# One layer kernel: transposes from DMA back to TensorE, and a last tile whose second FFN half, gate and final norm go block by block

## Time and profile before

| | |
|---|---|
| median of 3 runs | 3140.91 us (3126.2 to 3141.65) |
| profiled execution: time | 3140.91 us |
| its span, slowest core (core 4) | 3139.2 us |
| spans of the 8 cores | 3113.1 to 3139.2 us |
| TensorE busy (matmuls) | 3069.9 us, 98% of the span |
| VectorE, ScalarE, GpSimd busy | 58%, 37%, 21% |
| DMA | 659 MB, mean 210 GB/s |

### The profile page before, as it was taken

The page is one execution under the profiler, slowest core; times in us unless marked ns, Lnnn a source line. Parts: engine busy times, 40 slices in busy tenths (PEclk is TensorE's granted clock), DMA queues, the critical chain, the costliest instruction groups (busy, mean ns, idle before and its releaser), DMA issues.

```text
span 3139.2 us, 46426 instructions; the slowest of 8 cores (3113.1 to 3139.2 us)
## 1 busy us (share of the span) xinstructions
PE 3069.9 (98%) x15344; PEld 1438.5 (46%) x15344; DVE 1834.3 (58%) x3681; ACT 1150.9 (37%) x1781; POOL 654.5 (21%) x601
## 2 busy tenths in 40 slices
PE   5999998999999999999999999999999999999998
PEld 2444444444444444444444444444444444444443
DVE  4755655746657376564746657375564746656344
ACT  4563534423333343333323333342333323332333
POOL 2421301411313022130212313022130312313000
PEclk8789999999999999999999999999999999999999
DMA  8858684755767657666665667657666665766552
GB/s 266 239 177 278 218 258 141 269 169 194 225 210 245 193 194 234 204 226 190 232 199 201 230 203 247 191 192 236 204 226 191 226 206 199 231 195 209 183 184 81
DMA packets 280248, 659.07 MB, mean 210 GB/s; under 512 B 179536, under 2 KB 179792, under 8 KB 229840
## 3 DMA queue, kind: packets, MB, share of 16 engines
q1 hardware_dynamic: 280016, 656.11, 64.9%
HBM read 554.32 MB, written 60.82 MB: 196 GB/s over the span
## 4 chain that ended last, share of the span: by engine, by line
PE 95%; DMA 2%; DVE 1%; issue 1%; ACT 1%; POOL 0%; DVEq 0%; SPq 0%; ACTq 0%; POOLq 0%
PE ps L625 92%; DMA stage<-wf 1%; PE ps L633 1%; DMA stage<-xT 1%; PE ps L949 0%; PE ps L813 0%; PE ps L777 0%; PE ps L815 0%; PE ps L825 0%; DMA stage<-wple 0%; ACT xsb L645 0%; DVE scr L727 0%; DVE scr L724 0%; DVE scr L730 0%; DMA xb<-x 0%
## 5 line engine op out<-in xcount | busy, mean ns | idle before, releaser
L625 PE MATMUL ps<-TG,ring 128*128 128x512 bf16 x5120 | 1160.9, 382 | 31.2 <-ACT ring L581 25.7
L625 PE MATMUL ps<-ring,TG 128*128 128x512 bf16 x4096 | 982.1, 385 | 11.3 <-DVE xb L1006 4.4
L625 PE MATMUL ps<-ring,hT 128*128 128x512 bf16 x4096 | 921.6, 379 | 0.0
L625 PEld LDWEIGHTS ps<-TG,ring 128*128 128x128 bf16 x5120 | 501.6, 98 | 633.7 <-issue 56.4
L625 PEld LDWEIGHTS ps<-ring,TG 128*128 128x128 bf16 x4096 | 402.7, 99 | 497.0 <-issue 65.1
L1069 DVE TENSOR_TENSOR hT<-rel 128x512 bf16<-128x512 f32 x491 | 404.2, 824 | 380.1 <-ACT rel L1065 375.6
L625 PEld LDWEIGHTS ps<-ring,hT 128*128 128x128 bf16 x4096 | 396.0, 98 | 456.4
L1065 ACT ACTIVATE rel<-ps 128x512 f32<-128x512 f32 x512 | 305.1, 596 | 711.2 <-PE ps L625 702.2
L733 POOL TENSOR_TENSOR qk<-scr 128x512 bf16<-128x512 f32 x128 | 174.5, 1363 | 1245.7 <-DVE scr L730 1245.7
L1092 DVE SCALAR_TENSOR_TENSOR xb<-ps,st,xb 128x512 f32<-128x512 f32 x288 | 214.8, 746 | 289.0 <-PE ps L625 285.8
L645 ACT ACTIVATE xsb<-xb 128x1024 bf16<-128x1024 f32 x200 | 210.2, 1051 | 367.7 <-DVE xb L1092 240.7
(11 more groups left out here) (79 smaller groups left out, 2014.4 us busy)
## 6 DMA issues: line engine op xcount, KB each, us to landing
ring<-wb SPq DMA_DIRECT2D x366, 1024.0 KB, 6.6
stage<-wf SPq DMA_DIRECT2D x104, 512.0 KB, 8.9
stage<-xT SPq DMA_DIRECT2D x64, 512.0 KB, 8.3
xb<-x SPq DMA_DIRECT2D x64, 512.0 KB, 8.3
out<-xb SPq DMA_DIRECT2D x64, 512.0 KB, 4.7
stage<-x SPq DMA_DIRECT2D x56, 512.0 KB, 11.6
wb<-ring SPq DMA_DIRECT2D x26, 1024.0 KB, 9.9
rot<-ROT SPq DMA_DIRECT2D x16, 512.0 KB, 6.0
```

Of the source, the lines that this page charges most:

```text
L625: r = e.matmul(out(), lhs(k), rhs(k), start=(start + k == 0), stop=(start + k == total - 1))
```

## The change

1. The DMA way of transposing is removed (`dmaT`, and its uses in `yT`, `outproj` and `gate`): all tiles take the TensorE way that tiles 0 to 2 took.
2. The limit `DMA_AHEAD` in the scheduler's model is removed: a DMA is taken as soon as SyncE, its inputs and its buffers are free.
3. Pools: `xsb` 4 to 2 buffers, `scr` 8 to 9, `st` 14 to 16. `sqsum` takes an `xsb` buffer of its own for its unused output; before, in `norm_T`, it wrote into the buffer that the cast then filled.
4. Last tile only (t = 15): in the second part of its FFN all four `w2` units are loaded first, and the groups go block by block (for each block both halves of the columns) where they went unit by unit. Its gate goes block by block as well, both halves of a block after each other, with the inverse norm of each block worked out by itself.
5. Last tile only: the add of the gated term is on VectorE alone, the square of the last norm is taken in halves of 512 columns, the last scaling is two instructions of 512 columns, and each half has a store of its own (256 KB).
6. In all gates the two matmuls of `p @ w_ple` are added before the eight of the gate, and they now also name the block's transposed residual as an input.
7. `gate(1)` starts at virtual time 306, not 290.

```diff
-DMA_AHEAD = 6.0
...
-                    if op.dma is not None and dma_free[0] > now + DMA_AHEAD:
-                        heapq.heappush(events, dma_free[0] - DMA_AHEAD)
-                        continue
...
-... qk=8, v=4, svn=2, ktok=2, PT=2, y=8, xsb=4, pT=1, stage=4,
-                rot=1, rel=3, gt=2, scr=8, st=14, psum=8, Sbf=2)
+... qk=8, v=4, svn=2, ktok=2, PT=2, y=8, xsb=2, pT=1, stage=4,
+                rot=1, rel=3, gt=2, scr=9, st=16, psum=8, Sbf=2)
...
             def yT(b, half, src):
-                if t >= 3:
-                    dmaT(lambda: ap(ymix)[:, 4 * half:4 * half + 4, b * 128:(b + 1) * 128], lambda: ap(src),
-                         [(src, 0)], [(ymix, (half, b))], vt[0] - 3, lambda: ("ty", src.slot), 131072)
-                    return
                 p = g.buf("psum")
...
-                            norm_T(t, b, N2T[t], INV2[t], vt[0], t >= 3)
+                            norm_T(t, b, N2T[t], INV2[t], vt[0])
...
+            sqsum(xx, lambda: stc(stb, b), (stb, ("ss", b)), vt)
             xs = g.buf("xsb")
-            sqsum(xx, lambda: stc(stb, b), (stb, ("ss", b)), vt, xs)
...
-            if by_dma:
-                dmaT(lambda: ap(dst)[:, :, b * 128:(b + 1) * 128], lambda: ap(xs), [(xs, 0)], [(dst, b)], vt - 3,
-                     lambda: ("tx", xs.slot), 262144)
-                return
...
+                if ts[-1] == NT - 1 and part == parts - 1:
+                    for dh in range(2):
+                        for fg in range(nf):
+                            w2(dh, fg)
+                    for b in range(NB):
+                        for dh in range(2):
+                            for fg in range(nf):
+                                ff2(ts[-1], b, dh, fg)
...
-                norm_T(t, b, n3, st, vt[0], 2 <= t < NT - 1)
+                norm_T(t, b, n3, st, vt[0])
...
+                g.add(mmgroup(lambda: ps(p2), lambda k: ap(pt)[:, k, cols], lambda k: wple[:, k, hsl], 2),
+                      [(pt, 0), (n3, b), c("wple0"), c("wple1")], [(p2, 0)], vt[0])
...
+                g.add({"dve": (0.69, fad)} if last else {"pool": (1.27, fad), "dve": (0.69, fad)},
+                      [(gt, 0), (xx, half)], [(xx, half)], vt[0], lock=("pool", "dve"))
...
+                for i in range(2):
+                    hs = slice(i * 512, (i + 1) * 512)
+                    g.add({"dve": (0.69, lambda e, hs=hs: e.scalar_tensor_tensor(
+                        out=ap(xx)[:, hs], in0=ap(xx)[:, hs], scalar=stc(so, 8 + b), in1=gfin[:, hs], op0=ALU.mult,
+                        op1=ALU.mult))},
+                        [(xx, i), (so, ("rs", b)), c("gfin")], [(xx, i)], vt[0], lock=("dve",))
+                    store(b, hs, "xs%d" % i, (i,))
+            if t == NT - 1:
+                for b in range(NB):
+                    for half in range(2):
+                        gated(b, half, True)
+                        half_sq(b, half)
+                    final_last(b)
...
-        gate(1, 290.0, 40.0)
+        gate(1, 306.0, 40.0)
```

More of the change, by code:

```diff
@@ L635, in transposes, with sqsum @@
             return {"pe": (n * MS, fn)}
[L637 to L644, removed]
+        def sqsum(xbuf, acc, racc, vt):
+            j = g.buf("xsb")
             g.add({"act": (t_act(1024) + 0.19, lambda e: e.activation(out=ap(j), in_=ap(xbuf), func=AF.Square,
@@ L1053, in ffn, with ffn_part @@
             for part in range(parts):
+                ffn_part(ts, vt, adv, part, parts, nu)
+        def ffn_part(ts, vt, adv, part, parts, nu):
+            if True:
                 h = {}
@@ new lines, in ffn_part, with w2, ff2 @@
+                W2 = {}
+                def w2(dh, fg):
+                    if (dh, fg) not in W2:
+                        W2[dh, fg] = load_unit("w2_%d_%d" % (dh, part * nf + fg), vt[0] - 15)
+                    return W2[dh, fg]
+                fb = {}
+                def ff2(t, b, dh, fg):
+                    u = w2(dh, fg)
+                    if fg == 0:
+                        fb[t, b, dh] = g.buf("psum")
+                    p = fb[t, b, dh]
+                    cols = slice(b * 128, (b + 1) * 128)
+                    hsl = slice(dh * 512, (dh + 1) * 512)
+                    g.add(mmgroup(lambda: ps(p), lambda k: ap(h[t, fg * 8 + k])[:, cols],
+                                  lambda k: ap(u)[:, k, :], 8, start=fg * 8, total=8 * nf),
+                          UB(u) + [(h[t, fg * 8 + k], 0) for k in range(8)], [(p, 0)], vt[0])
+                    adv(8 * MM)
+                    if fg == nf - 1:
+                        xx, s4 = X[t, b], INV2[t]
+                        g.add({"dve": (0.69, lambda e: e.scalar_tensor_tensor(
+                            out=ap(xx)[:, hsl], in0=ps(p), scalar=stc(s4, 8 + b), in1=ap(xx)[:, hsl],
+                            op0=ALU.mult, op1=ALU.add))},
+                            [(p, 0), (xx, dh), (s4, "inv")], [(xx, dh)], vt[0])
@@ new lines, in ffn_part @@
+                if ts[-1] == NT - 1 and part == parts - 1:
[6 more added lines that the diff above has]
+                                ff2(ts[-1], b, dh, fg)
+                else:
+                    for dh in range(2):
+                        for fg in range(nf):
+                            for t in ts:
+                                for b in range(NB):
+                                    ff2(t, b, dh, fg)
@@ L1126, in gate, with gated @@
             so = g.buf("st")
-            for half in range(2):
+            WG = {}
+            def gated(b, half, last=False):
                 hsl = slice(half * 512, (half + 1) * 512)
-                u = load_unit("wg%d" % half, vt[0] - 25)
-                for b in range(NB):
[L1131 to L1159, removed]
-                            out=ap(xx), in0=ap(xx), scalar=stc(so, 8 + b), in1=gfin[:, :], op0=ALU.mult,
-                            op1=ALU.mult))},
-                            [(xx, 0), (xx, 1), (so, ("rs", b)), c("gfin")], [(xx, 0), (xx, 1)], vt[0], lock=("dve",))
-                        r0 = t * TT + b * 128
-                        dma(lambda r0=r0: out_d[r0:r0 + 128, :], lambda xx=xx: ap(xx), [(xx, 0), (xx, 1)], [],
-                            vt[0] - 20, lambda xx=xx: ("xs", xx.slot), 524288)
@@ new lines, in gated @@
+                g.add({"act": (t_act(512) + .1, lambda e: e.activation(
+                    out=ap(gt), in_=ps(p), func=AF.Tanh, scale=stc(st, 12 + b)))},
+                    [(p, 0), (st, ("rsh", b) if last else "rsh")], [(gt, 0)], vt[0])
+                g.add({"dve": (0.69, lambda e: e.scalar_tensor_tensor(
+                    out=ap(gt), in0=ap(gt), scalar=1.0, in1=ps(p2), op0=ALU.add, op1=ALU.mult))},
+                    [(gt, 0), (p2, 0)], [(gt, 0)], vt[0])
+                fad = lambda e: e.tensor_tensor(out=ap(xx)[:, hsl], in0=ap(xx)[:, hsl], in1=ap(gt), op=ALU.add)
@@ new lines, in gated, with store @@
+                g.add({"dve": (0.69, fad)} if last else {"pool": (1.27, fad), "dve": (0.69, fad)},
+                      [(gt, 0), (xx, half)], [(xx, half)], vt[0], lock=("pool", "dve"))
+                adv(10 * MM)
+            def store(b, hs, key, parts):
+                xx = X[t, b]
+                r0 = t * TT + b * 128
+                dma(lambda: out_d[r0:r0 + 128, hs], lambda: ap(xx)[:, hs], [(xx, i) for i in parts], [],
+                    vt[0] - 20, lambda: (key, xx.slot), 524288)
@@ new lines, in final @@
+            def final(b):
+                xx = X[t, b]
+                sqsum(xx, lambda: stc(so, b), (so, ("ss", b)), vt[0])
+                g.add({"dve": (TINY, lambda e: e.tensor_scalar(
+                    out=stc(so, 4 + b), in0=stc(so, b), scalar1=1.0 / D, scalar2=EPS, op0=ALU.mult, op1=ALU.add))},
+                    [(so, ("ss", b))], [(so, ("ms", b))], vt[0])
+                g.add({"pool": (1.0, lambda e: e.tensor_tensor(out=stc(so, 8 + b), in0=stc(so, 4 + b),
+                                                              in1=NEGH[:, 0:1], op=ALU.pow))},
+                      [(so, ("ms", b)), c("NEGH")], [(so, ("rs", b))], vt[0])
+                g.add({"dve": (1.28, lambda e: e.scalar_tensor_tensor(
+                    out=ap(xx), in0=ap(xx), scalar=stc(so, 8 + b), in1=gfin[:, :], op0=ALU.mult, op1=ALU.mult))},
+                    [(xx, 0), (xx, 1), (so, ("rs", b)), c("gfin")], [(xx, 0), (xx, 1)], vt[0], lock=("dve",))
+                store(b, slice(0, D), "xs", (0, 1))
@@ L1168, in build @@
+            if t == NT - 1:
+                for b in range(NB):
+                    for half in range(2):
+                        gated(b, half, True)
+                        half_sq(b, half)
+                    final_last(b)
+            else:
+                for half in range(2):
+                    for b in range(NB):
+                        gated(b, half)
+                        if half == 1:
+                            final(b)
         cache = {}
```

74 lines of the change are left out of this document (42 added, 32 removed).

## The result

The changed kernel takes 3257.83 us (median of 4 runs, 3238.97 to 3279.74), the kernel before 3133.55 us (median of 4). The ratio is 1.0377 with a 95% interval of 1.0312 to 1.0442: slower, as forecast, but by more: 3211 us and at most 3230 were forecast.

The account below looks back on a forecast made before the run. The prediction took TensorE to bound the kernel, saturated from 560 to 3128 us. Its terms summed as 3140.9 + 69.4 + 1 + 3 - 2 - 1 = 3211 us, with a range of 3190 to 3230 us.

Parts of the forecast that it names:

- What bounds the kernel: From 560 to 3128 us: TensorE is the bound, its waits 0.45 us in all; added TensorE work adds its whole length.
- 1248 transposes at 55.6 ns, 69.4 us: Transposes moved from DMA to TensorE, 96 for each of 13 tiles, all in the saturated stretch: 69.4 us added.
- Copies, +1 us: Copies of 208 transposed pieces from PSUM, hidden by idle time of VectorE and ScalarE: +1 us, bounds none to 20 us.
- the near-zero row: Low bound for late copies: no TensorE wait, as the saturated stretch has with its transposes of k; taken as +1 us.
- Late copies: Rival, steady tiles: tile 2's waits of 1.5 us, or twice that, in every tile; +20 to +40 us; chance 0.08.
- DMA limit, +3 us: Start: without the limit 5.0 MB more precede the weights, first matmul near 41 us, delay partly made good; +3 us.
- gate(1), -2 us: Between 500 and 560 us: with gate(1) later, gate(0) and tile 2's add come earlier; -2 us, bounds -8.4 to +8.4.
- The last tile, -1 us: End: the 11.0 us behind the last matmul shrink to about 10.2, VectorE may fall behind; -1 us, between -4 and +3.
- Slower at 0.97, range to 3230: Whole kernel: slower by more than about 0.5% at 0.97; 3190 to 3230 us, said to hold late copies' lower part.
- The clock rival: Rival, start: a denser start gives all cores the full clock sooner, 3211 - 18 = 3193 us; chance 0.14.

Follow-up runs that it names:

- Experiment 1: Kernel before with only the residual's transposes (outproj and gate) on TensorE, the mixer output's still by DMA; full-clock cores 3162.6 us, +45 us.
- experiment 4: Changed kernel with one line altered: a transpose of the mixer output also needs its TG buffer place before starting; full-clock cores 3189.7 us, ratio 1.0214.
- experiment 2: Kernel before with only the mixer output's transposes on TensorE, the residual's still by DMA; full-clock cores 3181.1 us, +63.5 us.
- experiment 8: Kernel before with the last tile's new order, gate(1) at 306, and TensorE's mixer-output transposes waiting for their TG place; full-clock cores 3110.1 us, ratio 0.9988.
- experiment 5: Kernel before with only the DMA limit of the scheduler's model removed; full-clock cores 3127.2 us, +10.7 us, ratio 1.0037.
- experiment 3: Kernel before with all transposes on TensorE and nothing else of the change; full-clock cores 3226.6 us, +109 us.
- experiment 10: Changed kernel with the copies of the transposed mixer output all on VectorE; full-clock cores 3240.2 us, 7 more than the changed kernel.

## Why the prediction was right or wrong

- **What bounds the kernel: right.** TensorE is the bound before and after, and work added to it came out in full.
- **1248 transposes at 55.6 ns, 69.4 us: right.** Experiment 1 has 54 ns for each (60 by its period), and experiment 4, where nothing waits, 193.5 - 188.2 = 5.3 us for 96 or 55 ns. The 275 ns of the Trainium skill, "TensorE: Matmul & The Clock Gate", Part 4, do not hold here; nor does the granted clock fall with transposes, it is 1.00 from 560 to 3227 us, though some 5 us of transposes in a tile of 197 could hardly show it. The gain that "VectorE: DVE Perf Modes" (Rules for kernel authors, again the Trainium skill) lets one expect didn't come: the DMAs that it would save were covered by TensorE's other work, which waited for 0.45 us in all before.
- **Copies, +1 us: wrong; this step failed.** It measured 40 us (63.5 - 23 in experiment 2; 43.9 in experiment 4, of which tile 2's share was there before). The forecast took the near-zero row as if PSUM buffers were to be had; in its place the runs showed transposed pieces that hold 6 to 7 of 8 banks until a `TG` buffer comes free. Two things went wrong in it. First, the two waits that it gave to tile 2 because they name a copy (0.8 + 0.7 us) are not both of tile 2: the one of 0.8 us stands at 161 us, while tile 2's run from 360 to 420 us (rows at experiment 8). Beside the one of 0.7 us behind L897 tile 2 has those on `rel` and `scr`, in the same order as the changed kernel's tiles; with all of them the bound was 13 x 3.3 = 43 us and not 20. Second, it put them down to first-time weights without looking at when transposes and copies start. "Late copies" stood as a rival with 20 to 40 us at 0.08; its size was right, which was luck, since its mechanism was wrong: the copying engines were idle and the target buffer was not there. The burst of eight transposing DMAs in the trace before said already that the pieces wait for it.
- **DMA limit, +3 us: mis-sized.** The first matmul came as worked out (39.9 us, forecast near 41), but most of the delay stayed: 10.7 us of 14. The later waits of the first 130 us, in which it was to be made good, hardly shrank: on core 2 they were 21.1 us before (130 - 84.57 busy - 24.38 to the first matmul) and 17.0 in experiment 5 (130 - 74.05 - 38.97). The term was within its bounds (-19 to +15.4).
- **gate(1), -2 us: right** (-2.3 to -3.3).
- **The last tile, -1 us: right in the stretch** (-0.45), and nothing that can be told from zero in the time.
- **The sum.** 109 (experiment 3) + 10.7 - 3.3 + 1 is 117 us, against 116 measured. Forecast were 70; of the 46 that were missing 39 are the copies' term and 8 the limit's. The same sum without the waits is what experiment 4 measured: 45 + 23 + 10.7 - 3.3 + 1 and -4 for tile 2's waits (experiment 8) are 72 us, against 72 measured (3189.7 - 3117.6).
- **Slower at 0.97, range to 3230: the sign was right.** The range claims to hold the lower part of the late-copies rival, but by that rival's own figures, 3231 to 3251, it holds none of it. The clock rival is borne out in part: in the runs compared 4 of 24 cores of the changed kernel are near 0.985, but two of these three runs have one, and the slowest core sets the time.

What stays open: experiment 10's 7 us, which lie ahead of the steady tiles (their period is the same, and the first long piece of 252 matmuls or more begins at 723.5 to 730.6 us on four full-clock cores, in the changed kernel at 715.3 to 724.6 on six), and why some cores keep a lower clock for the first 220 us.

## What to carry to other kernels

Ask first which engine is the bound. The DMAs cost the bound engine nothing here; the same transposes on TensorE added their whole length, and even without any wait for banks the kernel stayed 72 us slower (experiment 4).

When a transpose moves from a DMA to TensorE, count where its result waits: a DMA writes where the result is to stay, a transpose takes a PSUM bank until its copy has a target. Let the transpose wait for that target, not only the copy, and the banks stay free: here that one line was worth 44 us. If one tile of the old trace already does it the new way, take every wait of that stretch as the price, not only those that carry the name of the new operation.

## What the runs showed of the hardware beyond that

- Transposes of 128x128 in groups of 4 to 16 between matmuls cost 54 to 56 ns each on TensorE by starts and spans (experiments 1 and 4; 60 by experiment 1's period), about a quarter of the 216 ns of a matmul with 512 columns.
- The planner's limit on DMAs ahead sets when the first matmul comes: 37.5 to 40.4 us without it, 23 to 26 with 6 us, 20 to 23 with 2 us; on full-clock cores 3127, 3117 and (with experiment 8's edits, 3110 at 6 us) 3108 us.
- On one core of experiment 8 with a mean clock of 0.985 the granted clock was 0.79 from 40 to 140 us and 0.81 from 140 to 220, as means that lie between its levels of 1.2 and 2.4 GHz, with TensorE busy for 85.7 and 78.4 us; a core beside it had 0.91 and 0.99 at 81.5 and 78.6 us busy. How busy TensorE was does not tell the two apart.
